# Where a chunk-causal attention mask is written: VectorE memset in PSUM in place of a TensorE product

## What is computed

```python
def diff_attention(h, w_in, q_g, k_g, lq1, lk1, lq2, lk2, sub_g, w_out, lambda_init):
    q, k, v = jnp.split(h @ w_in, 3, axis=-1)          # H = 8 heads, two maps m of Dh = 64 each
    q = rms_norm(q.reshape(B, S, H, 2, Dh), q_g)
    k = rms_norm(k.reshape(B, S, H, 2, Dh), k_g)
    key_chunk = jnp.arange(S) // CHUNK                 # CHUNK = 64
    def block(args):                                   # one block of Q_BLOCK = 128 queries
        q_chunk = (bi * Q_BLOCK + jnp.arange(Q_BLOCK)) // CHUNK
        mask = key_chunk[None, :] <= q_chunk[:, None]
        s = jnp.einsum('bqhmd,bshmd->bhmqs', qi, k) * Dh ** -0.5
        s = jnp.where(mask, s, -jnp.inf)
        p = jax.nn.softmax(s, axis=-1)
        return jnp.einsum('bhqs,bshe->bqhe', p[:, :, 0] - lam * p[:, :, 1], v)
```

## Time and profile before

| | |
|---|---|
| median of 3 runs | 2988.28 us (2983.56 to 2990.59) |
| the profiled execution, its own time | 2985.84 us |
| its span in the trace | 2984.0 us |
| mean granted TensorE clock | 0.983 of full speed |
| busy: TensorE matmul, VectorE, ScalarE, GpSimd | 95%, 57%, 44%, 39% of the span |

### The profile page before, as it was taken

One profiled execution on the slowest core, in us unless ns is written; L12 is line 12 of the kernel. 1 busy time (PEld: TensorE's weight loads), 2 busy tenths in 40 slices (PEclk: granted clock), 3 DMA queues, 4 the chain that ended last, 5 costly groups with the idle time before them and its releaser, 6 DMA issues. The chain is left out here.

```text
span 2984.0 us, 42793 instructions
## 1 busy us (share of the span) xinstructions
PE 2845.7 (95%) x15296; PEld 2453.8 (82%) x15296; DVE 1705.7 (57%) x2432; ACT 1319.8 (44%) x2811; POOL 1156.7 (39%) x992
## 2 busy tenths in 40 slices
PE   7899999999999999977899799999999999999999
PEld 7898989888888989856678688888888888888887
DVE  5577776767677777757233244444444444444445
ACT  5566666666666666656222222222222222222222
POOL 4433334242424333213000455444455444545443
PEclk9999999999999999979899899999999999999999
DMA  6642424242423323110335411111113411111111
GB/s 247 243 142 90 156 81 153 96 151 94 147 98 116 130 93 133 35 66 6 115 125 192 155 57 55 51 49 56 56 49 148 164 49 56 56 56 49 56 50 57
DMA packets 167596, 296.84 MB, mean 99 GB/s; under 512 B 10512, under 2 KB 117008, under 8 KB 151056
## 3 DMA queue, kind: packets, MB, share of 16 engines
q1 hardware_dynamic: 163056, 278.04, 27.9%
q10 hardware_dynamic: 4384, 16.78, 1.4%
HBM read 244.45 MB, written 50.33 MB: 99 GB/s over the span
## 5 line engine op out<-in xcount | busy, mean ns | idle before, releaser
L1656 PE MATMUL banks<-u,w_hi 128*128 128x512 f32 x2048 | 632.8, 390 | 10.4 <-POOL w_lo L1456 10.4
L291 PE MATMUL proj<-w_hi,u_ring 128*128 128x384 f32 x2048 | 590.7, 348 | 8.8 <-issue 3.7
L1656 PEld LDWEIGHTS banks<-u,w_hi 128*128 128x128 f32 x2048 | 385.6, 188 | 91.0 <-POOL w_lo L1456 10.8
L1461 POOL TENSOR_TENSOR b_lo<-w_raw,b_hi 128x1024 fp32r<-128x1024 f32 x96 | 252.7, 2638 | 480.1 <-ACT b_hi L1531 480.1
L1656 PE MATMUL banks<-u,w_lo 128*128 128x512 f32 x1024 | 399.3, 390 | 0.0
L291 PEld LDWEIGHTS proj<-w_hi,u_ring 128*128 128x128 f32 x2048 | 376.8, 189 | 11.7 <-issue 6.1
L1580 DVE SCALAR_TENSOR_TENSOR hid<-banks,relu 128x512 f32<-128x512 f32 x128 | 88.5, 691 | 510.1 <-ACT relu L1549 510.1
L451 ACT ACTIVATE p_all<-scores,bias 128x1024 f32<-128x1024 f32 (+7 forms) x384 | 331.1, 864 | 90.5 <-DVE bias L429 46.1
L321 POOL TENSOR_TENSOR qk_rs<-qk_var,minus_half 128x4 f32<-128x4 f32 x128 | 129.7, 1013 | 607.4 <-DVE qk_var L315 607.4
L1593 DVE TENSOR_TENSOR y<-banks,y 128x1024 f32<-128x1024 f32 x224 | 272.0, 1220 | 152.8 <-PE banks L1640 152.8
L1640 PE MATMUL banks<-b_hi,a_hi 128*128 128x512 f32 x896 | 348.6, 389 | 0.3 <-issue 0.3
(11 more groups left out here) (120 smaller groups left out, 5347.2 us busy)
## 6 DMA issues: line engine op xcount, KB each, us to landing
u_ring<-u_scratch SPq DMA_DIRECT2D x112, 1024.0 KB, 5.2
w_raw<-in_mlp_w SPq DMA_DIRECT2D x128, 512.0 KB, 4.0
u_scratch<-u_ring SPq DMA_DIRECT2D x16, 1024.0 KB, 4.2
w_raw<-in_a_w_in SPq DMA_DIRECT2D x96, 128.0 KB, 4.6
p_all<-in_x SPq DMA_DIRECT2D x16, 512.0 KB, 4.2
rows_scratch<-o_sum SPq DMA_DIRECT2D x128, 64.0 KB, 1.6
o_in<-rows_scratch SPq DMA_DIRECT2D x16, 512.0 KB, 5.0
x_res<-in_x SPq DMA_DIRECT2D x16, 512.0 KB, 5.7
```

The costliest lines, as they stand in the source:

```text
L291: last = pe.matmul(proj[:, 0:3 * HD], u[:, part, kt, :], w[:, kt, :], start=(kt == 0 and part == 0 and w is w_hi), stop=(kt == KT - 1 and ...
L1461: pool.tensor_tensor(b_lo[:, p % BS], FULL_B[p], b_hi[:, p % BS].bitcast(F32), ALU.subtract)\
L1656: last = pe.matmul(banks[:, (Y_BANKS + e) % 8, :], w[:, j % 2, kt, :], u[:, n * TPB:(n + 1) * TPB, kt, :], start=(kt == 0 and w is w1_hi a ...
```

## The change

TensorE no longer issues the mask product: the `q_hi` product starts the accumulation over the bank's whole width. VectorE, once the piece is scored, writes -1e30 into the 64 x 64 square of the score bank with a memset, and waits for that memset before it takes the maximum. The memset stands in every step and map, in the piece that holds the last bank. The two mask tables, their four memsets and TensorE's wait for them go.

```diff
@@ pe_scores
-                    masked = bank == banks_of(t) - 1
-                    if masked:
-                        pe.matmul(scores[:, at, width - DH:width], mask_l[:, :], mask_r[:, :],
-                                  start=True, stop=False, skip_group_check=True)
                     pe.matmul(scores[:, at, 0:width], q_hi[:, m, rows], k_s[h % 2][:, m, keys],
-                              start=not masked, stop=False, skip_group_check=True)
+                              start=True, stop=False, skip_group_check=True)
@@ dve_max
             dve.wait_ge(scored, piece_count(a, m, k))
+            if first + banks == banks_of(t):
+                dve.memset(piece[0:DH, keys.stop - keys.start - DH:], MASKED).then_inc(masked, 1)
+                dve.wait_ge(masked, 2 * a + m + 1)
             if np == 1:
@@ the start of VectorE's program
-                dve.memset(mask_l[:, :], 0.0).then_inc(consts_set, 1)
-                dve.memset(mask_r[:, :], 0.0).then_inc(consts_set, 1)
-                dve.wait_ge(consts_set, 2)
-                dve.memset(mask_l[0:1, 0:DH], 1.0).then_inc(consts_set, 1)
-                dve.memset(mask_r[0:1, :], MASKED).then_inc(consts_set, 1)
...
-                dve.wait_ge(consts_set, 6)
+                dve.wait_ge(consts_set, 2)
```

More of the change, by code:

```diff
@@ L171, in attention_steps @@
         ident = sb("ident", [P, P])
-        mask_l = sb("mask_l", [P, P], BF16)
-        mask_r = sb("mask_r", [P, DH], BF16)
         g_q_raw = sb("g_q_raw", [P, 1])
@@ L230, in attention_steps @@
             sem("scored"), sem("piece_max"), sem("bias_set"), sem("exp_done"))
+        masked = sem("masked")
         z_summed, z_inverted, c_set = sem("z_summed"), sem("z_inverted"), sem("c_set")
@@ L951, in _ @@
                 pe_turn_qk(pe, NT - 1)
-                pe.wait_ge(consts_set, 4)
                 def late_values(a):
```

## The result

The changed kernel takes **3008.66 us** (median; 3006.67 to 3012.07) against 2988.24 us before: ratio 1.007, 95% interval 1.0057 to 1.0083. That is 20.4 us more; 11.8 were forecast. 3008.7 lies inside the range of 2986 to 3011, near its upper end, and just past the forecast's own band of +6 to +20 us. The profiled executions differ by 3009.7 - 2985.84 = 23.9 us, of which the spans show all (3007.9 - 2984.0).

The account below looks back on a forecast made before the run. TensorE was taken to bound steps 2 to 7, a loop through VectorE's row steps 10 to 15. The terms summed to 122 D - 10.2 = +11.8 us on 2985.8, rounded to 2998 us; range 2986 to 3011 us.

Parts of the forecast that it names:

- the forecast's own band: Whole kernel: memset delay between 0.13 and 0.25 us, so +6 to +20 us; chance 55%.
- the third rival: VectorE's memset is long, like an operation that reads PSUM: above 0.25 us, +20 to +28 us, 3009 us; chance 12%.
- D: Time by which a memset delays everything behind it on VectorE, wait included: 0.18 us, ends 0.07 and 0.31.
- What bounds which step: Heads 0 to 6: TensorE bounds steps 2 to 7 (-1.32 us), 8 and 9 tie, VectorE's row bounds 10 to 15 (+12 D).
- The rival that TensorE bounds the big steps too: Steps 2 to 15, heads 0 to 6: 28 products a head come back; -17 us in all, 2969 us; chance 13%.
- One sign: Steps 10 to 15: about 78.1 for 75.9 us, L512's waits for `pt_lo` growing over 0.4 us in each.
- The price of a mask product: TensorE: 0.11 us start to start for each of 256 products, returned only where TensorE is the bound.
- Steps 8 and 9, 0 and 1: Heads 0 to 6: + D for steps 8 and 9 together, + D for step 0, 0 for step 1.
- The last head: No projections, one chain: 24 D - 0.96 = +3.4 us.
- 2 D in 8 steps: Last head, big steps: VectorE works through to the awaited `pt_lo`, so each step grows by 2 D.
- 8 x (D - 0.12): Last head, small steps: the chain takes the product away and adds a memset, in 8 steps.
- Table memsets and the dropped wait: Removing four table memsets saves nothing, as VectorE then waits 3.48 us for ScalarE; TensorE's wait was met long before.

Follow-up runs that it names:

- the first experiment: The changed kernel without its memset and without the mask product, the 64 x 64 square left unmasked: 2976.28 us, ratio 0.9969 to the kernel before.

## Why the prediction was right

The direction and the mechanism came out; the size was half of the measured one, and that the time lies inside the range is in good part luck. +20.4 us is in the band of the third rival (D above 0.25 us, 3009 us), for which the range had been drawn up to 3011. But its cause is not what the runs show: D was 0.23 us at most. The largest part of the gap is the granted clock in the last head, for which the sum has no term.

**What bounds which step:** right, and the runs show it from both sides. Steps 2 to 7 answer to TensorE alone (-1.41 us without the products, 0.0 for one memset or two); steps 10 to 15 answer to VectorE alone (-0.1 and +2.46). The rival that TensorE bounds the big steps too fell with the first experiment: 10 us in place of 28. One sign failed in part: the waits for `pt_lo` were to grow by more than 0.4 us in each of steps 10 to 15, and at `t` = 14 it was 0.13. The step grew as said, but TensorE's other new waits lie earlier in it, for `k_s` and `p_all`, which hang on the same row of VectorE.

**The price of a mask product:** forecast 0.11 us, 1.32 us a head in steps 2 to 7; measured 1.41, so 0.12. The figure of about 25 ns in the Trainium skill ("TensorE: Matmul & The Clock Gate", section "Back-to-back issue gap") would have given 0.3 us a head, and these rows refuse it. The same section calls its figures those of a single matmul and says that at few columns they leave out the weight load; each of the 256 mask products had one, busy for 0.10 us.

**The price of a memset, D:** forecast 0.18 us everywhere; measured 0.23 behind an instruction whose end the next one used to overlap, and 0.12 behind `k_s`. In steps 10 to 15 there are eight of the first kind and four of the second, 8 x 0.23 + 4 x 0.12 = 2.32 us; they came to +2.34 us, for 2.16. The term was near by luck: the pair of memsets of the earlier trace rows has the cost of a memset that a memset waits for (0.20 in PSUM), and a maximum behind it starts sooner (0.14), while the lost overlap of 0.09 was left out.

**Steps 8 and 9, 0 and 1:** + D forecast for the first pair, +0.63 measured. I had taken TensorE to be the later one at `t` = 9; it was so by less than a tenth, and two D of 0.23 went past that. For steps 0 and 1 together, 0.18 forecast, 0.1 measured. The head came to 1.67 us in place of 1.20, and seven heads to 11.7 in place of 8.4.

**The last head:** here the size was off, "2 D in 8 steps" and "8 x (D - 0.12)", +3.4 us for 9.0. The chain was read rightly in the big steps: 2 D = 0.36 a step forecast, 0.32 measured in steps 8 to 14 at full clock. In the whole head it was put too high, 3.4 for 1.5 us at an almost full clock. What the term lacked was TensorE's clock. The trace of before already had it at 0.83 there, and I treated durations as fixed. In the profiled pair, 23.9 us apart, 12.1 are missing from the sum: 5.6 in the last head, 2.8 in single places (half-clock stretches in heads 0 and 4 among them), 3.3 in the terms of the steps above, and 0.4 outside. Why the clock falls at one wait and not at the next stays open: heads 1, 2, 5 and 6 had the longer waits as well and kept 1.00.

**Table memsets and the dropped wait:** no gain, as said.

## What to carry to other kernels

An engine that is busy for 98% of a stretch can still not be its bound: ask which of its waits recurs in each turn of the loop, and follow the loop once round. Work moves well from the full engine to the half-empty one only in those steps where the full one sets the pace; here the same edit wins 1.4 us a head in steps 2 to 7 and loses 3.0 in steps 8 to 15, and choosing it by step turned +20 into -10 us. A small operation's price is start to start with its neighbours, with the wait and the overlap it breaks; its busy time of 0.11 us was half of the 0.23.

## What the runs showed of the hardware

Added matmuls made a part shorter: with 8 + 4 unneeded products a step, the 138.18 us of the last head became 134.20 and its granted clock rose from 0.83 to 0.94, and in the changed kernel 147.13 became 135.68. In this part, where TensorE waits for others and the clock was already below full, longer waits thus cost more than their length; in heads 1, 2, 5 and 6, at 1.00, they did not.

A memset into PSUM behind a maximum that reads PSUM starts only at its end (1.22 us start to start, 1.22 busy), a memset into SBUF 0.05 us before it, and another reading operation 0.09 us before it. The same holds behind the combination, which reads and writes SBUF: at `t` = 11 the memset starts 1.69 us after it for 1.69 busy, where the maximum used to start after 1.60. Behind `k_s`, which writes partitions 64 to 127 of SBUF, neither a maximum nor a memset started before its end (0.46 and 0.44 us for 0.43 busy). The Trainium skill, "VectorE: DVE Perf Modes", section "Two Vector instructions with no wait between them", has a rule of this kind: an instruction is held until all earlier ones have finished if its input or output starts in another quarter of the partitions than the last one of the same memory. It agrees for `q_lo` to `k_s` to the next maximum (0.51 us start to start for 0.48 of busy time, and 0.46 for 0.43). It does not give the PSUM memset behind the maximum, since its output starts at partition 0, like that of the memset before it, and there the measurement stands.
